# Later folds and inner vectors, outputs ahead of the rounding, an earlier row fetch and a reordered tail in the expert stage of a fused encoder layer

## What is computed

```
g_sel = argmax(h @ w_group + b_group)             # one of 4 groups
e1, e2 = top2 of (h @ w_expert + b_expert) inside that group
w = softmax of the two logits * softmax(h @ w_group)[g_sel]
y[token] = sum over its two experts of w * ((silu(x @ w1[e]) * (x @ w3[e])) @ w2[e])
out = layer_norm(ALPHA * h + y, ln2_g, ln2_b)     # ALPHA = 2 ** 0.25
```

## Time and profile before

| | |
|---|---|
| median of 3 runs | 2135.28 us (2131.71 to 2135.75) |
| the profiled execution: its own time | 2134.49 us |
| its span, first to last instruction | 2132.7 us |
| TensorE busy | 2049.1 us (96%) |
| VectorE busy | 1555.0 us (73%) |
| ScalarE busy | 1192.5 us (56%) |
| granted TensorE clock, mean | 0.995 of full speed |
| moved by DMA | 613 MB, mean 288 GB/s; 410 to 430 GB/s in most slices of the expert stage |

### The profile page before, as it was taken

One profiled execution on the slowest core, in us unless ns is written; L12 is line 12 of the kernel. 1 busy time (PEld: TensorE's weight loads), 2 busy tenths in 40 slices (PEclk: granted clock), 3 DMA queues, 4 the chain that ended last, 5 costly groups with the idle time before them and its releaser, 6 DMA issues.

```text
span 2132.7 us, 27841 instructions
## 1 busy us (share of the span) xinstructions
PE 2049.1 (96%) x10774; PEld 1669.2 (78%) x10774; DVE 1555.0 (73%) x1498; ACT 1192.5 (56%) x967; POOL 135.7 (6%) x92
## 2 busy tenths in 40 slices
PE   8999999999999999999999999999999999999996
PEld 8998888899999998887887767667777666766663
DVE  7656664453646375454769999999999999999987
ACT  5445653333333323334346777777777777777773
POOL 1000000000000000001000111011110111011010
PEclk9999999999999999999999999999999999999998
DMA  6554335655454544667779999999999999999993
GB/s 215 158 140 158 118 119 185 209 181 170 147 177 146 169 157 155 220 216 256 227 286 366 410 426 427 426 427 427 424 426 426 420 422 422 417 415 421 410 426 159
DMA packets 143693, 613.47 MB, mean 288 GB/s; under 512 B 19057, under 2 KB 31489, under 8 KB 116257
## 3 DMA queue, kind: packets, MB, share of 16 engines
q1 hardware_dynamic: 137760, 601.14, 73.2%
q0 software_dynamic: 5856, 11.26, 1.5%
HBM read 612.87 MB, written 24.13 MB: 299 GB/s over the span
## 4 chain that ended last, share of the span: by engine, by line
PE 64%; DMA 12%; DVE 11%; issue 8%; ACT 3%; POOL 1%; POOLq 0%; DVEq 0%; ACTq 0%
PE ps L2023 18%; PE ps L2004 15%; DMA raw<-in_w_dram 7%; DVE wl L801 6%; PE ps L1152 5%; PE ps L1153 5%; DMA xrows<-xscr,rowno 4%; PE ps L2381 4%; PE ps L1149 4%; ACT wh L641 2%; DVE yall L973 2%; PE ps L2136 2%; PE ps L1174 1%; PE ps L2096 1%; PE ps L2109 1%
## 5 line engine op out<-in xcount | busy, mean ns | idle before, releaser
L801 DVE TENSOR_TENSOR wl<-raw,wh 128x2048 fp32r<-128x2048 f32 x320 | 720.4, 2286 | 72.0 <-ACT wh L641 71.0
L641 ACT ACTIVATE wh<-raw 128x2048 fp32r<-128x2048 f32 x320 | 604.4, 1912 | 184.6 <-PE ps L1153 82.0
L1578 DVE TENSOR_TENSOR wl<-raw,wh 128x2048 fp32r<-128x2048 f32 (+1 forms) x168 | 379.7, 2263 | 286.5 <-ACT wh L1382 286.4
L1382 ACT ACTIVATE wh<-raw 128x2048 fp32r<-128x2048 f32 (+1 forms) x168 | 317.9, 1894 | 447.4 <-DMA raw<-in_w_in_dram 276.4
L1152 PE MATMUL ps<-wh,xg 128*128 128x512 f32 x776 | 329.8, 425 | 33.7 <-DVE wl L801 33.4
L1153 PE MATMUL ps<-wl,xg 128*128 128x512 f32 x776 | 303.7, 391 | 0.0
L2004 PE MATMUL ps<-hth,wh 128*128 128x272 f32 (+1 forms) x896 | 259.7, 290 | 3.2 <-DVE wl L1578 1.8
L2004 PE MATMUL ps<-htl,wh 128*128 128x272 f32 (+1 forms) x896 | 255.8, 285 | 0.0
L2004 PE MATMUL ps<-hth,wl 128*128 128x272 f32 (+1 forms) x896 | 255.5, 285 | 0.0
L1149 PE MATMUL ps<-raw,xg 128*128 128x512 f32 x496 | 222.9, 592 | 0.0
L1152 PEld LDWEIGHTS ps<-wh,xg 128*128 128x128 f32 x776 | 145.9, 188 | 86.0 <-DVE wl L801 38.3
(11 more groups left out here) (369 smaller groups left out, 2918.0 us busy)
## 6 DMA issues: line engine op xcount, KB each, us to landing
raw<-in_w_dram SPq DMA_DIRECT2D x192, 2048.0 KB, 16.9
raw<-in_w_in_dram SPq DMA_DIRECT2D x103, 1024.0 KB, 5.1
raw<-in_w_pa_dram SPq DMA_DIRECT2D x16, 1024.0 KB, 5.0
raw<-in_w_pb_dram SPq DMA_DIRECT2D x16, 1024.0 KB, 5.1
raw<-in_w_out_dram SPq DMA_DIRECT2D x16, 1024.0 KB, 5.1
raw<-in_w_ukv_dram SPq DMA_DIRECT2D x8, 1024.0 KB, 5.4
yscr<-zeros SPq DMA_DIRECT2D x4, 1024.0 KB, 8.4
yrow<-yscr SPq DMA_DIRECT2D x4, 1024.0 KB, 19.6
```

The costliest lines, as they stand in the source:

```text
L641: nc.scalar.activation(wh2[:, x % HELD, :], raw_of(turn, x), ACT.Copy).then_inc(s_wh2, 1)
L801: nc.vector.tensor_tensor(wl_of(turn, x), raw_of(turn, x), wh2[:, x % HELD, :].bitcast(F32), ALU.subtract).then_inc(s_wl2, 1)
L1382: nc.scalar.activation(wh[:, n % RING1, 0:c], raw1[:, n % RING1, 0:c], ACT.Copy).then_inc(s_wh, 1)
L1578: nc.vector.tensor_tensor(wl[:, n % RING1, 0:c], raw1[:, n % RING1, 0:c], wh[:, n % RING1, 0:c].bitcast(F32), ALU.subtract).then_inc(s_wl, 1)
```

## The change

Six edits, all in the expert stage:
1. TensorE: `mix` moves from k = 0 to k = 1 and from k = 12 to k = 13 (in the first pair, with `early`, it stays at 14).
2. ScalarE and VectorE: `sigmoid` and `hidden` move with it.
3. ScalarE: `outputs` stands ahead of the `hi` of its step, at k = 7 and k = 19 (23 in the last pair), instead of behind it.
4. POOL: in its loop the fetch of rows stands ahead of both scatters.
5. Tail, data: ScalarE copies `xb0` in plain order to `xn0` at k = 23 of the last pair, TensorE reads that; the sum of tile 1's two choices moves from VectorE to POOL.
6. Tail, order: `stream_back` and `last_pair_back` take one bank at a time; the two halves of the last output release their banks apart (`s_half_out`); for tile 1 the two alternate; VectorE waits for POOL's sum only before tile 1.

```diff
@@ pool_experts @@
             def pairs(first, end):
                 with pool.Fori(first, end) as p:
+                    rows(p + 1, p)
                     scatter(p, 0)
-                    rows(p + 1, p)
                     scatter(p, 1)
@@ rows_there, on POOL @@
+                for r in range(2):
+                    pool.wait_ge(s_y[2 + r], 16 * rounds)
+                pool.wait_ge(s_yy, TT * rounds - 1)
+                nc.gpsimd.tensor_tensor(acc[:, 1, :], acc[:, 1, :], yrow[:, 1, 1, :], ALU.add).then_inc(s_yy, 1)
@@ pair of scalar_experts @@
+                    if k == 7 and not first:
+                        outputs(turn, x, 2 * turn - 1, 1, turn - 1)
+                    if k == (23 if last else 19):
+                        outputs(turn, x, 2 * turn, 0, turn)
                     if x + HELD != HELD or not early:
                         hi(turn, x + HELD)
-                    if k == 0 and not first:
+                    if k == 1 and not first:
                         sigmoid(2 * turn - 1)
-                    if k == 7 and not first:
-                        outputs(turn, x, 2 * turn - 1, 1, turn - 1)
-                    if k == 12 and not early:
+                    if k == 13 and not early:
                         sigmoid(2 * turn)
-                    if k == (23 if last else 19):
-                        outputs(turn, x, 2 * turn, 0, turn)
+                    if k == 23 and last:
+                        act.wait_ge(s_back, 16 * rounds)
+                        nc.scalar.activation(xn0[:, :].rearrange("q (p k) -> q k p", k=KD), xb0[:, :, :],
+                                             ACT.Copy).then_inc(s_own[0], 1)
@@ last_rest and one_round of vector_experts @@
-                m.then_inc(s_ye[1], 1)
+                    m.then_inc((s_half_out, s_ye[1])[c], 1)
-                choices(0, rounds)
+                choices(rounds)
                 last_rest(turn + PAIRS - 1, rounds)
-                choices(1, rounds)
@@ pair of tensor_experts @@
-                    if k == 0 and not first:
+                    if k == 1 and not first:
                         mix(turn - 1, j - 1, 1)
-                    if k == (14 if early else 12):
+                    if k == (14 if early else 13):
@@ end of one_round of tensor_experts @@
-                pe.wait_ge(s_back, 16 * rounds)
-                stream_back(0)
+                pe.wait_ge(s_own[0], rounds)
+                for c in range(4):
+                    stream_back(0, c)
+                pe.wait_ge(s_half_out, rounds)
+                for c in range(2):
+                    last_pair_back(0, c)
                 pe.wait_ge(s_ye[1], last + 1)
-                last_pair_back(0)
-                pe.wait_ge(s_own, rounds)
-                stream_back(1)
-                last_pair_back(1)
+                for c in range(2, 4):
+                    last_pair_back(0, c)
+                pe.wait_ge(s_own[1], rounds)
+                for c in range(4):
+                    stream_back(1, c)
+                    last_pair_back(1, c)
```

More of the change, by code:

```diff
@@ L319, in moe_trunk @@
         xb0 = place("xb0", [P, KD, P], 139264)
+        xn0 = place("xn0", [P, D_MODEL], 81920)
         xrows = place("xrows", [P, KD, P], 98304)
@@ L407, in moe_trunk @@
         s_yh = sem("s_yh")
+        s_half_out = sem("s_half_out")
         s_ye = [sem(f"s_ye{i}") for i in range(2)]
@@ L414, in moe_trunk @@
         s_stc = sem("s_stc")
-        s_own = sem("s_own")
+        s_own = [sem(f"s_own{i}") for i in range(TT)]
         s_cmb = sem("s_cmb")
@@ L718, in pair @@
                         nc.scalar.activation(xn1[:, :].rearrange("q (p k) -> q k p", k=KD), xs[:, 1, :, :],
-                                             ACT.Copy).then_inc(s_own, 1)
+                                             ACT.Copy).then_inc(s_own[1], 1)
                     for q in range(GQ):
@@ L950, in hidden_split, with choices @@
                                         ALU.subtract).then_inc(s_hxl, 1)
-            def choices(t, rounds):
+            def choices(rounds):
                 for r in range(2):
-                    dve.wait_ge(s_y[2 * t + r], 16 * rounds)
-                nc.vector.tensor_tensor(acc[:, t, :], acc[:, t, :], yrow[:, t, 1, :], ALU.add).then_inc(s_yy, 1)
+                    dve.wait_ge(s_y[r], 16 * rounds)
+                nc.vector.tensor_tensor(acc[:, 0, :], acc[:, 0, :], yrow[:, 0, 1, :], ALU.add).then_inc(s_yy, 1)
             def last_rest(turn, rounds):
@@ L1050, in normal @@
                                                ALU.add).then_inc(s_fin, 1)
-            dve.wait_ge(s_yy, TT * (more + 1))
+            dve.wait_ge(s_yy, TT * more + 1)
             for c in range(3):
@@ L1058, in vector_experts @@
             dve.wait_ge(s_acc, 1)
+            dve.wait_ge(s_yy, TT * (more + 1))
             for c in range(4):
@@ L1243, in pair, with stream_back, last_pair_back @@
                             gather(turn + 1, q, (s_hp, j if q < 2 and not first else j + 1))
[L1245 to L1257, removed]
+            def stream_back(t, c):
+                own_tile = (xn0, xn1)[t]
+                nc.tensor.matmul(ps[:, FINAL_BANK[t][c], :], ident[:, :], own_tile[:, 512 * c:512 * (c + 1)],
+                                 start=True, stop=False, skip_group_check=True)
+            def last_pair_back(t, c):
+                nc.tensor.matmul(ps[:, FINAL_BANK[t][c], :], selt[:, P * t:P * (t + 1)], yall[:, 512 * c:512 * (c + 1)],
+                                 start=False, stop=True, skip_group_check=True).then_inc(s_cmb, 1)
             def one_round(turn, rounds, early=False):
```

## The result

Median 2168.47 us (2167.6 to 2169.16) against 2133.54 for the kernel before on the same chip: ratio 1.0162, 95% interval 1.0149 to 1.0176, +34.9 us. The forecast was 2155.3: the sign was right, the time lies above the range. The spans differ by 2167.4 - 2132.7 = 34.7 us.

A forecast was written before the change was run, and what follows sets the result against it. Transfers and compute were held within 2 us per pair, with compute setting the pace after the change: 2134.5 + 24.4 (14 pairs) + 1.2 (last pair) - 4.8 (tail) = 2155.3 us; forecast's bounds 2141 to 2164, full range 2128 to 2164.

The forecast's parts named there:

- Outputs ahead: Each pair, k = 7 and k = 19: TensorE's next rounded unit starts 1.3 and 1.2 us later.
- fold one unit later: Each pair, k = 13 and k = 1: TensorE waits 0.9 and 0.3 us for differences the fold used to cover.
- Sigmoid and inner vector: Sigmoid and `hidden` following the fold: `hx` ready 1 to 1.5 us before its use, cost nil.
- Sum for a pair: Expert pairs: 60.4 + 2.2 + 1.5 - 1.1 = 63.0 us, taken as 62.4; over 14 pairs +24.4 us.
- last pair: Last expert pair: first half takes +2.2 us, about 1 us of TensorE's weight waits goes; +1.2 us.
- the fetch: POOL's rows fetch ahead of scatters: TensorE's 10.3 us of waits go, 0.74 per pair, about 1.1 in the walked one.
- the tail: After the last expert matmul: plain reading of tile 0 and alternating tasks of tile 1 gain 4.8 us, 29.6 instead of 34.4.
- the sum on POOL: Tail, tile 1's sum on POOL: costs nothing up to 7 us; the skill's 4.5 us leaves the forecast unchanged.
- Transfers keep the pace: Rival: later differences stay hidden under the transfer queue, so only the tail counts, 2129.7 us; chance 0.13.
- More even loads: Rival: earlier release of the odd unit brings late pairs to the early pace, 9.6 us less, 2120.1 us; chance 0.08.
- Half of it: Rival: only k = 7 costs, +1.1 us per early pair and 0 in late ones, 2139.7 us; chance 0.07.
- Above: Rival: `hx` late too, by 0.5 us in both halves, 14 us more, 2169 us; chance 0.05.

The follow-up runs named there:

- folds back: The changed kernel with folds, sigmoid and hidden put back to k = 0 and 12; outputs ahead, fetch and tail stay: 2144.43 us, ratio 1.0045.
- outputs back: The changed kernel with outputs put back behind the rounding on ScalarE; later folds, fetch and tail stay: 2130.53 us, ratio 0.9987.
- rest ahead: The changed kernel with output_rest also moved ahead of the difference of its step on VectorE: 2130.96 us, ratio 0.9987.
- the first experiment: The kernel before with one edit, outputs ahead of the rounding of their step on ScalarE: 2188.82 us, ratio 1.024.

## Why the prediction was right and wrong

**Right, the chain.** "Outputs ahead" and "fold one unit later" were walked at 1.3 + 1.2 and 0.9 + 0.3 us; each without the other, against compute's pace of 59.1, they measure 2.4 and 1.3, together 62.74 - 59.1 = 3.6 where I had 3.7. Sigmoid and inner vector cost nothing: in the pairs of the changed kernel TensorE has no wait for `hx`.

**Wrong, "Sum for a pair".** It fails twice. First, I walked 63.0 and took 62.4 on the guess that waits are met twice. The pace without the clock is 878.4 / 14 = 62.74, near the walk: 4.8 us over 14 pairs. Second, I priced the new waits of 1.8 and 2.1 us by their length alone. The granted clock fell behind them in 10 of 14 pairs, and 3.4 us at half speed cost 1.2 more each: 11.6 us, for which neither the sum nor a rival had a term. Without the falls the time is 2158.2 us, inside the range; it is this term that puts it outside. The 0.995 mean clock of the kernel before showed full speed in all its windows of this stage, but with waits for the difference of 30.3 / 28 = 1.1 us on average; the change has 63.2 / 40 = 1.6. The average is no sign by itself: with the folds back it is 54.9 / 28 = 2.0 and there is one fall. But waits of 2 us on TensorE were new ground and should have had a bound of their own, which would have carried the range's upper end past 2164.

**Wrong, last pair.** +1.2 forecast; start and last pair together gave 1.5 - 2.7 = -1.2. Why the last pair gained was not tried; that its waits for weights ended, as they did everywhere, fits.

The difference adds up: 4.8 + 11.6 - 2.4 = 14.0, against 34.7 - 20.8 = 13.9.

**Right, the fetch,** in that the wait for rows goes, and in its 0.7 to 1.1 us for a compute-bound pair. Alone it brings nothing, since transfers bound the sum.

**Right, the tail.** 29.6 us forecast, 29.5 measured, and -4.7 alone.

**Right, the sum on POOL.** 4.52 us, done at 2144.5, before VectorE asks at about 2146.7. The Trainium skill, GPSIMD Engine Reference, section 3.1 Elementwise, has 4497 ns for it, and the trace agrees; with the sum back on VectorE, in the kernel with fetch and tail alone, the time is 1.0 us longer, within the intervals.

**The rivals.** "Transfers keep the pace" is false for the whole change and true of nearly every part: fetch first, tail alone, outputs back and rest ahead all sum to 849.7 to 851.0 us, whatever compute's pace between 59.1 and 60.4. A mean of 60.7 us is the pace from which a loss is paid, and then in full: folds later alone sum to 856.0, outputs ahead with the fetch run at 61.5, which is 14 x 0.8 = 11 us, both edits together at 62.74, which is 878.4 - 849.2 = 29.2 us (the last two without the clock's part). "More even loads" is false: no order took less than 848.6 us for the pairs. "Half of it" is false for the change; 2144.4 with the folds back is the nearest to it (its price of 1.1 counts the fold's 0.9 in, though it is said to be that of k = 7 alone). "Above" has the measured time nearly to the microsecond, 2169, and that is luck: it has `hx` come late, and no wait for `hx` is in the trace.

**What was looked for** came: landing down to 10.7 us, GB/s down (403 against my 412), waits for weights and rows gone, TensorE's wait for the difference up to 63 us against my 75, periods of 62 to 63 us wherever the clock held.

**Open.** Why equal waits bring falls in one order and hardly any in another: the first experiment and "folds back" differ only in fetch and tail, and have 11 falls and 1. Whether the small matmuls of the fold hold the clock down or merely stand there when it is down for longer was not tried apart. And why DMA engines that are busy throughout move 425 GB/s in the early pairs and 418 in the late ones.

## What to carry to other kernels

Where compute and transfers run within 2 us of each other per round, single edits tell little: gains are swallowed (fetch first, nothing), a small loss is nearly free (folds, 1.3 us per pair), and the same loss is paid in full once another (outputs, 2.4) has used up the room: one by one, with the fetch first, they cost some 2 and 11 us without the clock's part, together 29. So sum the walks against the slower pace before believing either. A new wait on TensorE has its length as one price and may have a second, what follows it at half clock; here 22 of 84 waits of 1.8 to 2.2 us had it, and no run says which will. If the wait must stay, small matmuls in it whose result nobody reads bought the second part back in both kernels where they were tried. And when an operation is moved ahead on one engine, move its partner on the next engine too, or the chain gets longer instead of shorter.

## What the chip did that I had not expected

- Waits of 1.8 to 2.1 us were followed by a granted clock of 0.5, in some cases and not in others: 10, 11 and 1 times behind 28 waits each. While it lasted a matmul of 512 columns took 0.63 us instead of 0.39 and the fold 3.51 instead of 1.89. In the expert stage of all runs it lasted 10.2 us where the fold's small matmuls began within 1.2 us of its start (8 times), and 3.4 us where they began 1.6 us after it or later (18 times). Twelve small matmuls in the wait removed it: 2168 to 2158 us, and 2189 to 2156 us.
- One edit alone (+55 us) cost more than the bundle that contains it (+35). In the bundle the fold starts 4.0 to 5.2 us after the clock fell, and each fall was 3.4 us and not 10. But the later folds are not what makes the bundle cheaper: with them back it takes 2144 us with a single fall, and why the falls are gone there is open.
- The landing time of the weight loads told the bound, and the DMA share did not: 10.7 us median where compute sets the pace, 19.0 where the transfers do, at DMA shares of 0.98 and 1.00.
